# Expert gathers of a PEER layer: 64 tokens x 2 slots per gather, weights of 128x64 in two column tiles

## The reference, cut to what matters

```python
def peer(h, norm_g, w_q, sub_keys, u, v):
    xn = rmsnorm(h, norm_g).reshape(T, D)
    q = (xn @ w_q).reshape(T, PEER_HEADS, PEER_DKEY)
    s1 = einsum('thd,nd->thn', q[..., :half], sub_keys[0]); s2 = ...  # second half
    v1, i1 = top_k(s1, 16);  v2, i2 = top_k(s2, 16)
    cs, ci = top_k((v1[..., :, None] + v2[..., None, :]).reshape(T, 8, 256), 16)
    experts = (e1 * N_KEYS + e2).reshape(T, 8 * 16)
    gates = softmax(cs).reshape(T, 8 * 16)
    z = einsum('td,ted->te', xn, u[experts])            # one row of u per token and slot
    act = gelu(z) * gates
    return einsum('te,ted->td', act, v[experts])        # one row of v per token and slot
```

## Time and profile before

| | |
|---|---|
| median of 3 runs | 1639.29 us (1638.07 to 1639.36) |
| profiled execution | span 1790.2 us; the profile has no time for this execution beside its span |
| PE / DVE / POOL / ACT busy | 1418.7 / 1134.1 / 1060.9 / 276.2 us |
| moved by DMA | 647.10 MB, of them 536.94 MB by the gathers |

### The profile page before, as it was taken

The page is one execution under the profiler, slowest core; times in us unless marked ns, Lnnn a source line. Parts: engine busy times, 40 slices in busy tenths (PEclk is TensorE's granted clock), DMA queues, the critical chain, the costliest instruction groups (busy, mean ns, idle before and its releaser), DMA issues.

```text
span 1790.2 us, 16346 instructions
## 1 busy us (share of the span) xinstructions
PE 1418.7 (79%) x5036; PEld 840.4 (47%) x5036; DVE 1134.1 (63%) x2871; ACT 276.2 (15%) x762; POOL 1060.9 (59%) x1030
## 2 busy tenths in 40 slices
PE   7987688998998678888679677888577876687766
PEld 7876444664665245544346244454336532233322
DVE  2655775765676686675558686675464858664445
ACT  1221011211111110121111111122111111111110
POOL 0005654776767655677666655577675666666664
PEclk9998898998999889998889889899798988898887
DMA  9677989999999999999999999999899899999998
GB/s 340 259 306 287 330 321 325 398 412 387 363 413 411 409 356 407 368 392 360 379 393 393 396 359 379 361 360 350 305 385 346 301 393 349 371 355 373 374 363 327
DMA packets 164241, 647.10 MB, mean 361 GB/s; under 512 B 18624, under 2 KB 18880, under 8 KB 151616
## 3 DMA queue, kind: packets, MB, share of 16 engines
q0 software_dynamic: 147456, 536.94, 78.9%
q1 hardware_dynamic: 16704, 109.17, 15.3%
HBM read 644.99 MB, written 1.05 MB: 361 GB/s over the span
## 4 chain that ended last, share of the span: by engine, by line
PE 45%; issue 15%; DVE 14%; another core or an unknown queue 12%; POOL 6%; ACT 5%; DMA 3%; ACTq 0%; POOLq 0%; DVEq 0%
PE acc L1456 23%; PE bank L1231 9%; DVE u_ring L860 6%; PE bank L1235 5%; POOL u_ring L431 3%; POOL v_ring L431 3%; ACT diag L1130 2%; PE bank L1211 2%; DMA u_ring<-in_u,idx_all 2%; PE bank L1409 1%; DMA v_ring<-in_v,idx_all 1%; ACT arena L955 1%; DVE xn L453 1%; ACT xT L940 1%
## 5 line engine op out<-in xcount | busy, mean ns | idle before, releaser
L1456 PE MATMUL acc<-v_ring,diag 128*128 128x512 f32 x1932 | 926.3, 641 | 226.2 <-ACT diag L1130 120.6
L431 POOL DMA_INDIRECT v_ring<-in_v,idx_all x512 | 533.7, 1042 | 411.8 <-PE acc L1456 198.9
L1456 PEld LDWEIGHTS acc<-v_ring,diag 128*128 128x128 f32 x1932 | 392.9, 206 | 737.5 <-issue 612.0
L431 POOL DMA_INDIRECT u_ring<-in_u,idx_all x512 | 525.2, 1026 | 306.3 <-issue 148.6
L860 DVE SCALAR_TENSOR_TENSOR u_ring<-u_ring,scp 128x1024 f32<-128x1024 f32 x272 | 319.3, 1218 | 105.3 <-DMA u_ring<-in_u,idx_all 99.2
L860 DVE SCALAR_TENSOR_TENSOR u_ring<-u_ring,xp 128x1024 f32<-128x1024 f32 x240 | 285.1, 1227 | 65.7 <-DMA u_ring<-in_u,idx_all 40.5
L874 DVE SCALAR_TENSOR_TENSOR act_w<-ez,gz 128x8 f32<-128x8 f32 x64 | 10.8, 169 | 242.9 <-ACT ez L1125 180.2
L1130 ACT ACTIVATE diag<-ident,act_w 128x128 f32<-128x128 f32 x483 | 148.4, 388 | 18.9 <-DVE act_w L874 8.3
L1235 PE MATMUL bank<-w_ring,xT 128*128 128x256 f32 x576 | 131.4, 389 | 4.9 <-ACTq L941 4.9
L1235 PEld LDWEIGHTS bank<-w_ring,xT 128*128 128x128 f32 x576 | 111.6, 195 | 23.3 <-ACTq L941 6.0
L1231 PE MATMUL bank<-xT,w_ring 128*128 128x128 f32 x896 | 112.8, 289 | 9.4 <-issue 8.0
(11 more groups left out here) (161 smaller groups left out, 973.8 us busy)
## 6 DMA issues: line engine op xcount, KB each, us to landing
w_ring<-in_wall SPq DMA_DIRECT2D x86, 1024.0 KB
u_ring<-in_u,idx_all POOLq DMA_INDIRECT x512
v_ring<-in_v,idx_all POOLq DMA_INDIRECT x512
u_ring<-in_wall SPq DMA_DIRECT2D x4, 1024.0 KB, 10.1
v_ring<-in_wall SPq DMA_DIRECT2D x3, 1024.0 KB, 8.9
arena<-in_wall SPq DMA_DIRECT2D x3, 1024.0 KB, 15.6
gains<-in_gains SPq DMA_DIRECT2D x5, 512.0 KB, 14.1
kept<-in_wall SPq DMA_DIRECT2D x2, 1024.0 KB
```

The lines of the kernel that those rows point to most:

```text
L431: nc.gpsimd.indirect_dma_start(out=ring[:, r, :], out_offset=None, in_=table, in_offset=bass.IndirectOffsetOnAxis(ap=idx_all[:, slot:slot ...
L1456: ins = M(acc[:, s], diag[:, r, :], v_ring[:, r, s], start=h_last and lo + n == 0 and r == 0, stop=not h_last and hi == ROUNDS and n == hi ...
```

## The change

It changes how tokens and slots lie on the 128 partitions during a round.

- A gather holds 2 slots of 64 tokens: partitions 0 to 63 one slot, 64 to 127 the next. The rows fetched in a phase are the same, and there are as many gathers.
- The 128 columns of tokens are two column groups. PE's weights for a gather are 128x64 (`diag` is made from `stack`, two 64x64 identities on top of each other) and its result goes to partitions 0 to 63 of `acc` for even places of the ring, 64 to 127 for odd ones; matmuls of the two groups alternate.
- The dots read `xrep`, the token rows repeated twice for each group. PE makes it by 8 matmuls of 64x512 (`replicate`) into `scp` and `tr`, ACT copies it to SBUF.
- Expert numbers and gates must be moved to the new places: DVE writes both to `flat`, PE rearranges them (`turn_slots`, 4 small matmuls per part into a bank that is otherwise for projections), DVE copies them to `idx_all` and `gate_all`. So the gates now come before the expert numbers are free, and DVE waits for PE.
- The v rows on DVE (rounds 12 to 15 of phases 0 to 2, and the last 5 rows) are gone: PE does all. The token's vector is never read from PSUM by the dots.

```diff
@@ DVE, pair_part: what stood in gate_part now stands before the indices @@
-                V.tensor_scalar(idx_all[...], en[...], float(layer * N_EXPERTS), None, ALU.add).then_inc(idx_ready, heads)
-            def gate_part(phase, p): ...
+                tick(V.tensor_scalar(flat[:, 0, 0:m], flat[:, 0, 0:m], float(layer * N_EXPERTS), None, ALU.add))
                 answer()
                 link(V.tensor_reduce(gsum[:, 0:heads], g3, AX.X, ALU.add))
                 link(V.reciprocal(gsum[:, 0:heads], gsum[:, 0:heads]))
                 link(V.scalar_tensor_tensor(out=g3, in0=g3, scalar=0.5, in1=over(gsum[:, 0:heads], TOPK), ...))
+                dve.sem_inc(slots_ready, 1)
+                turned = bank[count.banks % 2]
+                dve.wait_ge(slots_turned, count.parts)
+                V.tensor_copy(idx_all[:, first:first + m], turned[:, 0:m]).then_inc(idx_ready, heads)
+                link(V.tensor_copy(gate_all[:, first:first + m], turned[:, m:2 * m]))
+                dve.sem_inc(bank_read, 1)
@@ DVE, route @@
-                for c in range(2): V.tensor_scalar(scp[:, s], xp[:, t, s], xr[:, t:t + 1], None, ALU.mult)
+                link(V.tensor_scalar(xp[:, :], xp[:, :], xr[:, t:t + 1], None, ALU.mult))
+                dve.sem_inc(xn_ready, 1)
@@ DVE, gather @@
-                    tokens = scp[:, :] if phase + 1 == PHASES or lo + n < PSUM_ROUNDS else xp[:, t, :]
+                        if lo + n == 0 and r < PACK:
+                            dve.wait_ge(rep_read, PACK * phase + r + 1)
-                        V.scalar_tensor_tensor(out=u_ring[:, r, :], in0=u_ring[:, r, :], scalar=1.0, in1=tokens,
+                        V.scalar_tensor_tensor(out=u_ring[:, r, :], in0=u_ring[:, r, :], scalar=1.0, in1=xrep[:, r % PACK, :],
-                    for r in range(first_for_pe(first + n)): ...   # v rows on DVE
@@ ACT, gather @@
+                        act.wait_ge(u_used, RING + SLOTS * phase)
+                        for m in range(PACK):
+                            act.wait_ge(rep_full, PACK * phase + m + 1)
+                            A.activation(xrep[:, m, :], source[:, :], ACT.Copy).then_inc(rep_read, 1)
-                        A.activation(diag[:, r, :], ident[:, :], ACT.Copy,
+                        A.activation(diag[:, r, :], stack, ACT.Copy,
@@ PE @@
+            def turn_slots(p):
+                pe.wait_ge(bank_read, count.banks)
+                out = take_turn()
+                wait_next(slots_ready)
+                for c in range(PACK):
+                    for s in range(PACK):
+                        ins = M(by_token(y, s)[:, :, :, c], by_column(ident, c), x[:, :, :, s], start=True, stop=True)
+                ins.then_inc(slots_turned, 1)
+            def replicate(m):
+                for s in (slice(0, 512), slice(512, D)):
+                    for g in range(PACK):
+                        ins = M(by_token((scp, tr)[m % 2], g)[:, s], by_column(ident, m), xp[:, s], start=True, stop=True)
-                        for s in halves:
-                            ins = M(acc[:, s], diag[:, r, :], v_ring[:, r, s], ...)
+                    for q in range(0, RING, PACK):
+                        for half, s in enumerate(halves):
+                            for r in range(q, q + PACK):
+                                ins = M(by_token(acc, r % PACK)[:, s], diag[:, r, :], v_ring[:, r, s], start=False, ...)
```

More of the change, by code:

```diff
@@ L48 @@
 CHUNK = 2048
[L49 to L50 removed]
+PACK = 2
+TOK = P // PACK
 GELU_CUBE = 0.044715
@@ L144, in __init__ @@
         self.banks = 0
+        self.parts = 0
+        self.alone = -1
         self.transposes = 0
@@ L297, in build, with by_token @@
         block = ctx.enter_context(nc.Block())
-        def by_vector(n):
-            return VECTOR_ROWS * sum(m < n for m in VECTOR_ROUNDS)
-        def first_for_pe(n):
-            return VECTOR_ROWS if n in VECTOR_ROUNDS else 0
-        def worked_by_pe(n, r):
-            return n * RING + r + 1 - by_vector(n) - first_for_pe(n)
-        def rows_for_pe(phase, n):
-            return RING - LAST_ROWS if phase == PHASES - 1 and n == ROUNDS - 1 else RING
+        def by_token(a, c):
+            return a[c * TOK:(c + 1) * TOK]
         def run(rows_of, mixer, route):
@@ L589, in hgrn @@
                     if level % 2 == 0:
+                        count.banks += 1 if level < 4 else 0
                         yield
@@ L689, in attention @@
                 count.transposes += 1
+                count.banks += 2
                 yield
@@ L695, in attention @@
                 count.transposes += 2
+                count.banks += 1
                 yield
@@ L698, in attention @@
                 mask = amask[:, 0:3 * P] if t == 0 else amask[:, 3 * P:9 * P]
-                o = bank[(count.banks + 6) % 2]
+                o = bank[(count.banks - 1) % 2]
                 for j in range(NJH + 1):
@@ L863, in round_of @@
                     dve.wait_ge(u_used, at(RING, RING + (first + n + 1) * RING))
-                    gate = (first + n) * RING
+                    gate = (phase % 2 * ROUNDS + lo + n) * RING
                     gate = gate_all[:, gate:gate + RING] if i is None else gate_all[:, bass.ds(i * (GROUPS * RING) + gate, RING)]
@@ L1060, in rest @@
                     yield
-                    route_part(phase, p)
+                    route_part(p)
+                    count.banks += 1
                     yield
@@ L1093, in route @@
                 yield
-                route_part(phase, 0)
+                route_part(0)
                 queries(1)
+                count.banks += 1
                 queries(2)
@@ L1099, in route @@
                 yield
-                route_part(phase, 1)
+                route_part(1)
+                count.banks += 1
                 queries(3)
@@ L1384, in route @@
                 for n, (first, width, _, at) in enumerate(PIECES[layer]):
-                    transpose_part([xp[:, t, c:c + P] for c in range(first, first + width, P)], n, at)
+                    transpose_part([xp[:, c:c + P] for c in range(first, first + width, P)], n, at)
                 turn_of = {}
@@ L1465, in gather @@
                         pe.wait_ge(acc_read, phase)
-                    for s in halves if not h_last else ():
-                        M(acc[:, s], ident[:, :], h[:, t, s], start=True, stop=False)
+                    for s in halves:
+                        M(acc[:, s], ident, h[:, t, s], start=True, stop=False)
                 if hi - lo > GROUPS:
```

165 lines of the change are left out of this document (81 added, 84 removed).

## The result

The changed kernel takes 1675.02 us (median of 4 runs, 1672.6 to 1675.85), the kernel before, run beside it, 1638.73 us: a ratio of 1.0221, 95% interval 1.0207 to 1.0236. That lies above the range of 1622 to 1668 us. The sign was forecast as the likelier one; the size was not.

A forecast was written before the change was run, and what follows sets the result against it. The prediction took DMA traffic as the bound. Its terms, +11 opening, -9 and -2 PE's v rows, +3 SBUF vector and +1 end, sum to +4 us: 1643 us for the median, range 1622 to 1668 us.

The forecast's parts named there:

- What bounds: Whole kernel: DMA traffic, 647.10 MB at 413 GB/s or 1567 us, is the bound; no compute engine is near full.
- PE's v rows: A round's v matmuls take 7.0 instead of 14.0 us; -9 us at 200 to 300 us, -2 for all later holes.
- the hole at 200 to 300 us: Stretch of the earlier trace with DMA share 0.87, 13 us idle, where PE's v rows stand beside the next tile's mixer.
- rival C: Column tiles don't overlap, PE keeps 14 us a round: 1664 us; chance 0.13.
- The v rows on DVE: Rounds 12 to 15: removing DVE's 24 rows, 31 us of its time, gives nothing, as weights keep the DMA full.
- The opening: Start of the kernel: gates, turns and repeats delay first gather, first dots and u of round 2; +11 us, bounds +4 and +17.
- The token's vector from SBUF: Dots on SBUF rows slow POOL's gathers; nothing in phases 0 to 2, +3 us in phase 3, bounds 0 and +59.
- Rival D: POOL becomes the bound in phase 3, where dots run back to back in routing rounds: +28 instead of +3, 1668 us; chance 0.14.
- the prediction's own sign: In phase 3 a gather would take POOL 0.95 to 1.05 us if the forecast held.
- The +59: Upper bound for the SBUF vector in phase 3: 16 x 3.7 us, every round with dots back to back.
- The same steps in later phases: Turns and repeats after the opening lie under 20.3 us of traffic per round: nothing, up to +10 if DVE falls behind.
- The end: Last rows: PE takes the last pair and DVE two copies; +1 us, or +5 without overlap.

The follow-up runs named there:

- e5: The kernel before, unchanged, run again for a trace beside the changed kernel: 1638.72 us.
- e7: Changed kernel with the token rows repeated ahead of the second part's turn of the slots, and phase 0's ACT copies to xrep earlier: 1663.80 us.
- e3: The kernel before with VECTOR_ROUNDS empty, so no v rows on DVE in mid-phase: ratio 1.0236 to the kernel before, in an 1800 us session.
- e10: Same edit as e3, the kernel before with VECTOR_ROUNDS empty, measured again: ratio 1.0160 to the kernel before, in an 1800 us session.
- e15: Same edit as e3, the kernel before with VECTOR_ROUNDS empty, a third time: ratio 1.0209 to the kernel before, in an 1800 us session.
- e8: Changed kernel with e7's edit, and the last phase's dots reading the repeated rows in PSUM without ACT's copies to xrep there: 1652.92 us.
- e1: The kernel before, unchanged, run again for a second trace: 1807.5 us, in an 1800 us session.
- e11: Changed kernel with two loops swapped, so both halves of a slot follow each other on one column tile: 1847.33 us against 1802.31 for the kernel before.

## Why the prediction was wrong, step by step

*What bounds.* Right, and more so than written. The DMA queues bound the kernel before: at 399 to 411 GB/s from 150 us to the end. Dividing bytes by the rate and asking what is lost was the right sum. But the rate and the holes came from a trace whose time was 9% off the median, and I took the difference for something of the profiled execution alone. The prediction had the warning in its own figures: only 11 us were left for all holes, and yet it booked 11 back.

*PE's v rows, -9 and -2.* The mechanism was right, the gain mostly not there. The v matmuls of a round take 7.32 us against 14.00, and PE's busy time fell by 1386.9 - 1136.8 = 250 us, not 400; in phase 3 a round takes 10.02 us at the lower clock. Of the hole at 200 to 300 us nothing is in e5, so the 9 us were not to be had. Between 200 and 500 MB 4.2 us do come back, against the 2 forecast for later holes; no run shows whether they are PE's. The Trainium skill (TensorEngine Tiling (Array Packing), Key Properties) says that different tiles can run their weight loads and matmuls in parallel. The trace agrees with it, by 7.32 us, and rival C's doubt is gone.

*The v rows on DVE, nothing.* Not refuted in sum, but the reason was wrong for the kind of session it was read from: e3, e10 and e15 show them to be worth 29 to 42 us in 1800 us sessions. That removing them was free because PE got faster at the same time is the likely reading, and argued only.

*The opening, +11.* Each event was placed well: first gather forecast 139.8 and measured 139.27; first dot 173 and 165.97; u of round 2 at 198 and 194.61. The reference of 186.60 belongs to the other kind of session. In e5 that gather stands at 175.60, so the delay is 19.0 us, and 18.5 us are lost by 60 MB. But 16 x (1.33 - 0.94) = 6 of them are POOL's slow gathers in round 1, which belong to the vector. Without them some 12 are left: the term was right, though partly by luck, as its end was reckoned from the wrong reference. e7 shows that 11 us of the whole hang on where the repeats stand.

*The token's vector from SBUF, +3.* This is the step that failed: it measures about 24 us, and the 21 us more than priced are two thirds of the miss. It was priced near the rows in which dots wait one by one, and at nothing in phases 0 to 2, where "the weights give POOL room". In rounds 1 to 5 of the first phase there is no such room: POOL waits for nobody from 195 us on, and 6 us in round 1 and 7.5 in rounds 2 to 5 go with gathers of 1.33 and 1.13 us on the mean. In phase 3's rounds with routing 8 dots run back to back, up to 4 gathers of a round take 1.75 to 1.99 us, and POOL needs up to 23.8 us where transfers need 20.5: 10.2 us. The last figure is shown, by e7 against e8; the two of the first phase are worked out from traces, since e8 keeps the SBUF vector there and no run in a 1640 us session takes it away.

Rival D had this mechanism, with +28 us in phase 3 as its price, and got 0.14. It was not right either. Its bar, a mean gather over 1.1 us in phase 3, was not reached: 1.09 in the first eight rounds, 1.03 in all 16, which is within the 0.95 to 1.05 of the prediction's own sign. The argument against it, that a bound POOL spaces the rows and spaced dots cost little, holds for the plain rounds (0.97 us, the fence below; no loss by bytes). It fails where routing holds DVE for longer than a round's rows need to land.

The Trainium skill (SBUF — State Buffer, Who interferes with whom) says that a VectorE instruction with two SBUF inputs holds up only a GpSimd instruction that reads SBUF, and infers that the building of descriptors, which needs the write side, is spared. The trace shows gathers held up, 1.99 instead of 0.94 us. This agrees with the first if a gather counts as reading SBUF, since its row numbers lie there in `idx_all`, and is against the inference if not; no run here tells which. The +59 that the prediction worked out for 4 slow gathers in each of phase 3's rounds compares with the 10.2 measured there. POOL of the changed kernel in plain rounds:

```profile
1510.00:1630.00 120.00, 91.60 (x94) 0.74 1.03 410
```

*The same steps in later phases, nothing.* Right at 300 to 1290 us, where most of DVE's 63.3 us of waiting for turned slots cost no transfers: 410 GB/s stand there against 408 before. Wrong at the change to phase 3, which loses 6.2 us (3.7 in e8). The prediction had DVE wait for the round's v rows alone; 7.41 us of projections stand between them and the turn, DVE waits 11.18 us, and the dots behind it free POOL's places late. It is one of the prediction's own signs of being wrong, waits of DVE for `slots_turned` that delay POOL's u gathers, though not in every routing round.

*The end, +1.* The lag falls from 38.4 us at 580 MB to 37.0 at the end: 1.4 less instead of 1 more. DVE's five rows were slower than PE's last pairs.

*The sum again.* 12 for the opening, 24 for the vector (6 + 7.5 + 10.2), 6 at the change to phase 3, for the most part the turn, -4 up to it and -1.4 at the end: 37 us, as the two spans say. Against the forecast's terms that is +1 on the opening, +21 on the vector, +7 on what was to come back, +6 on a term put at nothing and -2 at the end. Rival D's 28 in place of the 3, with no gain, would have given 11 + 28 + 1 = +40, or 1679 us; that it comes near is luck, since of D's 28 us in phase 3 only 10 are there.

## What to carry to other kernels

Before a trace is priced, hold its span against the runs beside it: 9% more is not to be put down to the profiler, and a hole that only the longer execution has gives nothing back. Here the page itself had a mark of it, 12% of its chain under "another core or an unknown queue". Where one engine builds the transfers that bound a kernel, work out its round against the transfers' round in each kind of round, the crowded one first; here 19.8 against 20.5 us left 0.7 us of room, and one operand's place took up to 3 to 4. Freeing an engine that doesn't bound (250 us of PE) paid for 4 us at most, while what was done for it ahead of the first transfers counted in full. When a wait of one engine for another is put at nothing, count what stands ahead of the awaited step on that other engine: 7.41 us of projections, here.

## What the runs showed of the hardware

- The same kernel moves its data at 410 GB/s in some sessions (e5, 200 to 300 us) and at 306 to 376 on the mean of long stretches in others (e1), with slices up to 413, whole sessions at a time, profiled or not: 1640 and 1800 us. The cause isn't known. The Trainium skill (Perfetto Trace Analysis, Roofline) gives 358 GB/s as a core's share when both cores of a pair use the memory, and more for a core alone; the two levels would fit a neighbour that is busy in some sessions, but no run here shows one.
- An indirect gather takes POOL 0.94 us, and 1.99 beside back-to-back VectorE dots whose two inputs stand in SBUF. With one of the inputs in PSUM it takes 0.94 (e7 against e8: 19 and 2 of 128 gathers over 1.5 us).
- Float32 matmuls that alternate between two 64-column tiles of TensorE go at twice the pace of 128-column ones (7.32 against 14.00 us for 16), whether the two tiles alternate one by one or two by two (e11). In rounds where PE idles for 10 us first, at a granted clock of 0.68 of full speed on the mean of that stretch, the same 16 take 10.02 us.
